# Rotary halves exchanged by VectorE's shuffle instead of by a second set of products, in a two-layer streaming encoder on one core

## The reference

```python
def _rope(x, pos):
    half = x.shape[-1] // 2
    ...
    x1 = x[..., :half].astype(jnp.float32)
    x2 = x[..., half:].astype(jnp.float32)
    return jnp.concatenate([x1 * cos - x2 * sin, x2 * cos + x1 * sin], axis=-1).astype(x.dtype)
...
    q_nope, q_pe = q[..., :MLA_NOPE], _rope(q[..., MLA_NOPE:], pos)
    ckv = _rmsnorm(kv_lat, g_kv_lora)
    kpe = _rope(kpe_raw, pos)
```

## Time and profile before

| | |
|---|---|
| median of 3 runs | 1674.59 us (1674.06 to 1676.32) |
| the profiled execution, its own time | 1674.04 us |
| its span | 1672.2 us |
| busy: TensorE matmuls | 1639.2 us (98%) |
| busy: DVE, ACT, POOL | 1105.0 us (66%), 804.4 us (48%), 576.6 us (34%) |
| heads 0 to 7 | from about 80 us to about 262 us |

### The profile page before, as it was taken

The page is one execution under the profiler, slowest core; times in us unless marked ns, Lnnn a source line. Parts: engine busy times, 40 slices in busy tenths (PEclk is TensorE's granted clock), DMA queues, the critical chain, the costliest instruction groups (busy, mean ns, idle before and its releaser), DMA issues.

```text
span 1672.2 us, 31609 instructions
## 1 busy us (share of the span) xinstructions
PE 1639.2 (98%) x12240; PEld 1589.7 (95%) x12248; DVE 1105.0 (66%) x2047; ACT 804.4 (48%) x1502; POOL 576.6 (34%) x432
## 2 busy tenths in 40 slices
PE   9999999999999999999999999999999999999998
PEld 8989999999998999999999999899989999999998
DVE  5666655555655996587477689533358965874876
ACT  4465555454655654255144445545456541551443
POOL 4453446454553032022013357655550320220122
PEclk9999999999999999999999999999999999999999
DMA  7221223334323133233233322443241332332231
GB/s 193 77 62 53 59 76 98 79 96 108 81 63 80 52 102 114 64 101 104 74 90 88 86 68 69 118 114 89 58 116 52 101 106 71 100 103 76 77 100 58
DMA packets 282744, 145.45 MB, mean 87 GB/s; under 512 B 60334, under 2 KB 273004, under 8 KB 282596
## 3 DMA queue, kind: packets, MB, share of 16 engines
q1 hardware_dynamic: 278136, 136.27, 29.5%
q0 software_dynamic: 3616, 6.92, 1.6%
q10 hardware_dynamic: 844, 0.24, 0.1%
HBM read 130.69 MB, written 15.32 MB: 87 GB/s over the span
## 4 chain that ended last, share of the span: by engine, by line
PE 81%; DVE 11%; ACT 3%; issue 3%; DMA 1%; POOL 1%; SPq 0%; DVEq 0%; ACTq 0%
PE ACC L1269 39%; PE ACC L1682 7%; PE ACC L1684 7%; PE ACC L1683 7%; PE T L1269 3%; PE S L1269 2%; PE ACC L1549 2%; PE S L1524 2%; DVE SCO L2863 2%; DVE TOP L2860 1%; ACT PR L2114 1%; PE S L1684 1%; PE S L1682 1%; PE S L1683 1%; PE T L1537 1%
## 5 line engine op out<-in xcount | busy, mean ns | idle before, releaser
L3502 POOL TENSOR_TENSOR HF<-SG,U 128x576 f32<-128x576 f32 x44 | 65.1, 1478 | 498.4 <-ACT SG L2302 402.3
L1269 PE MATMUL ACC<-XGh,WH 128*128 128x288 f32 (+1 forms) x1008 | 227.6, 307 | 6.7 <-ACT U L2367 2.2
L3347 POOL TENSOR_TENSOR WL<-RAW,WH 128x1024 fp32r<-128x1024 f32 (+3 forms) x84 | 181.4, 2162 | 147.5 <-ACT WH L1989 147.2
L1269 PE MATMUL ACC<-XGh,WL 128*128 128x288 f32 (+1 forms) x1008 | 215.4, 295 | 0.0
L1269 PE MATMUL ACC<-XGl,WH 128*128 128x288 f32 (+1 forms) x1008 | 215.4, 295 | 0.0
L1989 ACT ACTIVATE WH<-RAW 128x1024 fp32r<-128x1024 f32 (+3 forms) x159 | 153.2, 971 | 79.6 <-PE ACC L1269 43.4
L1682 PE MATMUL ACC<-TB,WH 128*128 128x288 f32 x640 | 189.1, 295 | 0.6
L1684 PE MATMUL ACC<-TB,WL 128*128 128x288 f32 x640 | 188.8, 295 | 0.0
L1683 PE MATMUL ACC<-TB,WH 128*128 128x288 f32 x640 | 188.4, 294 | 0.0
L1269 PE MATMUL ACC<-HH,WH 128*128 128x288 f32 x1032 | 179.2, 295 | 0.0
L1269 PEld LDWEIGHTS ACC<-XGh,WH 128*128 128x128 f32 (+1 forms) x1008 | 159.2, 188 | 11.8 <-issue 3.2
(11 more groups left out here) (469 smaller groups left out, 4308.3 us busy)
## 6 DMA issues: line engine op xcount, KB each, us to landing
RAW<-in_w_gate_dram SPq DMA_DIRECT2D x44, 512.0 KB, 3.9
RAW<-in_w_up_dram SPq DMA_DIRECT2D x44, 512.0 KB, 4.6
RAW<-in_w_down_dram SPq DMA_DIRECT2D x32, 512.0 KB, 4.1
RAW<-in_w_in_even_dram SPq DMA_DIRECT2D x29, 512.0 KB, 5.0
RAW<-in_w_in_odd_dram SPq DMA_DIRECT2D x28, 512.0 KB, 4.4
RAW<-in_w_out_even_dram SPq DMA_DIRECT2D x16, 512.0 KB, 4.0
RAW<-in_w_down_dram SPq DMA_DIRECT2D x16, 384.0 KB, 3.5
RAW<-in_w_out_odd_dram SPq DMA_DIRECT2D x8, 512.0 KB, 5.2
```

The lines of the kernel that those rows point to most:

```text
L1269: ins = pe.matmul(out[0:m, 512 * b:512 * b + width], left, right[:, b * width:(b + 1) * width], start=(first and part == 0), stop=(last an ...
L3347: pool.tensor_tensor(WL[slot][:, 0:n], RAW[slot][:, 0:n], WH[slot][:, 0:n].bitcast(F32), ALU.subtract).then_inc(w_lo_pool, 1)
L3502: pool.tensor_tensor(HF[:, q, :], SG[:, q, :], U[:, q, :], ALU.mult).then_inc(h_out, 1)
```

## The change: no second product, a shuffle on VectorE

The columns of the rotary weights, the rows of COS and SIN and the cached keys are laid out so that both halves that change places lie within one group of 32 partitions (16 rows of one and 16 of the other). The product "ps" is gone, and VectorE exchanges the halves of "pe" in PSUM with a stream shuffle. Output tile 5 of heads 3 and 5 stands in slot 4. The key is rotated the same way, its unit is loaded twice as it is, and its columns are reordered as they are split. The store of the latents puts the rotated columns back in order.

```diff
+HALF_SWAP = [(i + SQUARE // 2) % SQUARE for i in range(SQUARE)]
...
-LATENT_TILES = {2: 4, 5: 5, 6: 6, 7: 7}
+LATENT_TILES = {2: 4, 4: 5, 6: 6, 7: 7}
...
-    "even": [("q", 0, 3), ("k", 0, 2), ("v", 0, 2), ("pe", 0, 3), ("ps", 0, 3), None, None, None],
+    "even": [("q", 0, 3), ("k", 0, 2), ("v", 0, 2), ("pe", 0, 3), None, None, None, None],
...
-    "first even": [("q", 0, 3), ("k", 0, 2), ("pe", 0, 3), ("ps", 0, 3), ("v", 0, 2), None, None, None],
+    "first even": [("q", 0, 3), ("k", 0, 2), ("pe", 0, 3), None, ("v", 0, 2), None, None, None],
...
-            unit("pe", g, cols=2 * QLT * P, end=("ps", g))
+            unit("pe", g, cols=QLT * P, end=("pe", g))
...
-            for n, w in enumerate(("k", "v", "pe", "ps", "q")):
+            for n, w in enumerate(("k", "v", "pe", "q")):
...
-    unit_dmas[("kp",)] = 3
+    unit_dmas[("kp",)] = 2
     for n in units.names:
         if n[0] == "pe":
-            unit_dmas[n] = 3 * QLT
+            unit_dmas[n] = 4 * QLT
...
+        def halves_apart(rows):
+
+            return rows.rearrange("p (s q i) -> p q s i", s=2, q=2)
...
-                        sp.dma_start(dst, pe).then_inc(loaded, 16)
-                        sp.dma_start(dsw[:, :, 0:half], pe[:, :, half:ROPE]).then_inc(loaded, 16)
-                        sp.dma_start(dsw[:, :, half:ROPE], pe[:, :, 0:half]).then_inc(loaded, 16)
+                        for h in range(2):
+                            first = (name[1] + h) * (HD + ROPE) + HD
+                            pe = halves_apart(wq[k * P:(k + 1) * P, first:first + ROPE])
+                            for q in range(2):
+                                dst = raw[:, k * P + h * ROPE + q * SQUARE:k * P + h * ROPE + (q + 1) * SQUARE]
+                                sp.dma_start(dst, pe[:, q]).then_inc(loaded, 16)
...
-            sp.dma_start(COS[:, :], a["cos"]).then_inc(rope_in, 16)
-            sp.dma_start(SIN[:, :], a["sin"]).then_inc(rope_in, 16)
+            for dst, src in ((COS, a["cos"]), (SIN, a["sin"])):
+                for o in range(0, P, SQUARE):
+                    rows = src[o // ROPE * ROPE:(o // ROPE + 1) * ROPE, :].rearrange("(s q i) c -> q s i c", s=2, q=2)
+                    sp.dma_start(dst[o:o + SQUARE, :], rows[o // SQUARE % 2]).then_inc(rope_in, 16)
...
-            for o in (0, ROPE):
-                sp.dma_start(CCK[:, KV_LORA + o:KV_LORA + o + ROPE], a["cache_mla_kpe"][0, 0]).then_inc(cc_in, 16)
+            for o in range(0, P, SQUARE):
+                sp.dma_start(CCK[:, KV_LORA + o:KV_LORA + o + SQUARE],
+                             halves_apart(a["cache_mla_kpe"][0, 0])[:, o // SQUARE % 2]).then_inc(cc_in, 16)
...
-                prepare(g, "ps", 0, QLT)
...
+                if name == ("kp",):
+                    old, new = rotary_columns(RAW[slot]), rotary_columns(WH[slot], turned=True)
+                    act.activation(new[:, :, 0], old[:, :, 0], ACT.Copy)
+                    act.activation(new[:, :, 1], old[:, :, 1], ACT.Copy).then_inc(w_hi, 1)
+                    return
...
-                act.wait_ge(acc_free, acc.made("ps", g))
+                act.wait_ge(acc_free, acc.made("pe", g))
...
+            def rotate(out, dst):
+
+                link(dve.tensor_tensor(two(dst), halves(out), two(COS[:, :]), ALU.mult))
+                link(dve.stream_shuffle(halves(out), halves(out), HALF_SWAP))
+                link(dve.tensor_tensor(halves(out), halves(out), two(SIN[:, :]), ALU.mult))
+                return dve.tensor_tensor(two(dst), halves(out), two(dst), ALU.add)
...
-            dve.tensor_tensor(two(YQ[lower, :]), halves(TT)[lower], two(COS[lower, :]), ALU.mult)
-            link(dve.tensor_tensor(two(YK[lower, 0:NT]), halves(TT)[upper], two(SIN[upper, :]), ALU.mult))
-            link(dve.tensor_tensor(YQ[lower, :], YQ[lower, :], YK[lower, 0:NT], ALU.add))
-            dve.tensor_tensor(BO[lower, 0, :], YQ[lower, :], RSTD[lower, :], ALU.mult).then_inc(kp_taken, 1)
-            dve.tensor_tensor(BO[upper, 0, :], YQ[lower, :], RSTD[lower, :], ALU.mult).then_inc(lat_ready, 1)
+            rotate(TT, YQ).then_inc(kp_taken, 1)
+            dve.wait_ge(kp_taken, 1)
+            dve.tensor_tensor(BO[:, 0, :], YQ[:, :], RSTD[:, :], ALU.mult).then_inc(lat_ready, 1)
...
-                    dve.tensor_copy(CKF[0:r, t, :], T[tr.at("lat", t) % 2][0:r, 0:KV_LORA + ROPE]).then_inc(t_free, 1)
+                    out = T[tr.at("lat", t) % 2][0:r, :]
+                    dve.tensor_copy(CKF[0:r, t, 0:KV_LORA], out[:, 0:KV_LORA])
+                    dve.tensor_copy(halves_apart(CKF[0:r, t, KV_LORA:KV_LORA + ROPE]),
+                                    out[:, KV_LORA:KV_LORA + ROPE].rearrange("p (q s i) -> p q s i", q=2, s=2)).then_inc(t_free, 1)
...
-                        ins = dve.tensor_tensor(two(rotated(g)), halves(out), two(COS[:, :]), ALU.mult)
-                    elif what == "ps":
-                        link(dve.tensor_tensor(halves(out), halves(out), two(SIN[:, :]), ALU.mult))
-                        dve.wait_ge(acc_free, acc.made("pe", g))
-                        ins = dve.tensor_tensor(two(rotated(g)), halves(out), two(rotated(g)), ALU.add)
+                        ins = rotate(out, rotated(g))
```

More of the change, by code:

```diff
@@ L341, in plan_attention @@
                 r, what, k0, k1, total = c
-                if k0 == 0 and what not in ("v", "ps") or (k0 == 0 and what == "v" and kind_of(r) != "mla"):
+                if k0 == 0 and what != "v" or (k0 == 0 and what == "v" and kind_of(r) != "mla"):
                     if kind_of(r) != "mla":
@@ L349, in plan_attention @@
                     else:
-                        unit("pe", r, cols=2 * QLT * P, end=("ps", r), in_slot=True)
+                        unit("pe", r, cols=QLT * P, end=("pe", r), in_slot=True)
                 if k1 == total:
@@ L354, in plan_attention @@
                         finished.append((what, r))
-                    elif what in ("q", "v", "ps"):
-                        finished.append(({"v": "kv", "ps": "pe"}.get(what, what), r))
+                    elif what in ("q", "v", "pe"):
+                        finished.append(({"v": "kv"}.get(what, what), r))
             if h < 16 and g is not None and s == k_job_slot(g) == 5:
@@ L845, in last_s, with rotary_columns @@
             return sc.made("s", h, TOK_TILES - 1, 1 if kind_of(h) == "diff" else 0)
+        def halves_apart(rows):
+            return rows.rearrange("p (s q i) -> p q s i", s=2, q=2)
+        def rotary_columns(tile, turned=False):
+            order = "p (m q s i) -> p m q s i" if turned else "p (m s q i) -> p m q s i"
+            return tile[:, :].rearrange(order, q=2, s=2, i=SQUARE // 2)
         def rows_of(t):
@@ L924, in unit_loads @@
                 if w == "kp":
-                    c, r = Q_LORA + KV_LORA, ROPE // 2
-                    return [(0, ROPE, tiles(w_even, 0, DT, c, ROPE)), (ROPE, r, tiles(w_even, 0, DT, c + r, r)),
-                            (ROPE + r, r, tiles(w_even, 0, DT, c, r))]
+                    return [(o, ROPE, tiles(w_even, 0, DT, Q_LORA + KV_LORA, ROPE)) for o in (0, ROPE)]
                 if w == "qi":
@@ L1412, in _ @@
             pe.wait_ge(kp_taken, 1)
-            pe.wait_ge(cc_in, 16 * 3)
+            pe.wait_ge(cc_in, 16 * 5)
             out = rotate_to_tokens(("cc",))
@@ L1444, in prepare @@
                     latent_product(("q", g), ("q", g), 0, P, k0, k1, QLT, QGh, QGl, HALF)
-                elif what in ("pe", "ps"):
-                    latent_product((what, g), ("pe", g), 0 if what == "pe" else QLT * P, P, k0, k1, QLT, QGh, QGl, HALF)
+                elif what == "pe":
+                    latent_product(("pe", g), ("pe", g), 0, P, k0, k1, QLT, QGh, QGl, HALF)
                 else:
@@ L2531, in unit_lo @@
                 slot = slot_of[name]
+                if name == ("kp",):
+                    old, new, high = rotary_columns(RAW[slot]), rotary_columns(WL[slot], turned=True), rotary_columns(WH[slot], turned=True)
+                    dve.tensor_tensor(new[:, :, 0], old[:, :, 0], high[:, :, 0].bitcast(F32), ALU.subtract)
+                    dve.tensor_tensor(new[:, :, 1], old[:, :, 1], high[:, :, 1].bitcast(F32), ALU.subtract).then_inc(w_lo, 1)
+                    return
                 dve.tensor_tensor(WL[slot][:, 0:n], RAW[slot][:, 0:n], WH[slot][:, 0:n].bitcast(F32),
@@ L2629, in _ @@
             begin("kp")
-            dve.wait_ge(rope_in, 16 * 2)
+            dve.wait_ge(rope_in, 16 * 8)
             dve.wait_ge(kp_done, 1)
-            lower, upper = slice(0, ROPE), slice(ROPE, P)
-            dve.tensor_tensor(two(YQ[lower, :]), halves(TT)[lower], two(COS[lower, :]), ALU.mult)
-            link(dve.tensor_tensor(two(YK[lower, 0:NT]), halves(TT)[upper], two(SIN[upper, :]), ALU.mult))
-            link(dve.tensor_tensor(YQ[lower, :], YQ[lower, :], YK[lower, 0:NT], ALU.add))
-            dve.tensor_tensor(BO[lower, 0, :], YQ[lower, :], RSTD[lower, :], ALU.mult).then_inc(kp_taken, 1)
```

(4 more changed lines are left out.)

10 lines of the change are left out of this document (2 added, 8 removed).

## The result

The changed kernel takes 1683.95 us (median of 4 runs, 1681.82 to 1688.74), the kernel before beside it 1674.76: a ratio of 1.006, 95% interval 1.0043 to 1.0078. It is slower by some 9 us. The prediction was 1678.1 us with a range to 1681.5: the right side, and too little. The profiled execution took 1681.82 us with a span of 1680.0, so 7.8 us over the profiled one of before.

A forecast was written before the change was run, and what follows sets the result against it. TensorE, busy 98%, bounds the kernel, but the chain leaves it behind the removed products. +1.0 + 1.2 + 1.2 + 0.1 = +3.5 us on 1674.04, put on the runs' median: 1678.1 us, range 1673.0 to 1681.5.

The forecast's parts named there:

- The shuffle: VectorE's exchange of halves in each rotation: taken as 0.77 us from the stream transpose's row, bounds 0.4 and 1.3 us.
- Head 1: All four rotation operations stand ahead of tile 3's row minima, delaying ScalarE and head 2's scores: +1.0 us.
- Heads 3 and 5: Tile 4's row minima come 2.40 us late, and the next head's first product 1.2 us late: +1.2 us per head.
- Prologue: TensorE's turn stays within 0.3 us, its idle time becomes 3.0 us, second latent copies cost: +0.1 us, between -0.3 and +0.8.
- the key and SyncE's DMAs: Key rotation and extra DMA issues ahead of later loads: costed at nothing, up to +1 us if the DMAs' slack is gone.
- Rival 3: TensorE's clock falls behind idle stretches in prologue and heads 1, 3, 5: +2.4 us once to +9.6, 1680.5 to 1687.7; chance 0.07.
- a dear shuffle: A shuffle of 1.3 us, its excess counted three times, in heads 1, 3 and 5: +1.6 us.
- one fall: One drop of TensorE to 1.2 GHz behind an idle stretch, making the next product take 2.4 us more.
- rival 2: About no change: one of three delays is real, slack in ScalarE and VectorE absorbs the others; 1675 to 1677, chance 0.27.

The follow-up runs named there:

- the first experiment: Changed kernel with unread products on TensorE in its holes (prologue, heads 1, 3 and 5), VectorE's order and all waits kept: 1679.52 us, ratio 1.002.
- The last experiment: The first experiment with the lower half of head 0's odd queries moved on VectorE from slot 0 to slot 4: 1677.92 us, ratio 1.0014.
- The eighth: Changed kernel with 20 unread products on TensorE in the prologue's hole alone, other holes left open: 1682.55 us, ratio 1.0043.
- the second experiment: Changed kernel with the rotation of heads 2, 4 and 6 cut in two on VectorE around the next tile's row minima: 1678.38 us, ratio 1.0013.
- the eleventh: The ninth without its unread products, same orders, holes left open: 1672.68 us, ratio 0.9982.
- the ninth: The fifth with unread products of heads 3 and 5 moved to tile 3's score bank and head 0's odd lower half to slot 4: 1670.95 us, ratio 0.9975.
- fifth: Changed kernel with the rotation cut in two, VectorE reordered in the prologue and heads 3 and 5, and remaining holes filled with unread products: 1675.40 us, ratio 0.9998.
- sixth: Kernel before the change with only two VectorE reorderings, in the prologue and for output tile 6 in heads 3 and 5: 1675.62 us, ratio 0.9997.

## Why the prediction was wrong

**The shuffle: right.** Forecast 0.77 us, measured 0.76 in all five places, and the load of its mask takes 0.01. The Trainium skill, "VectorE: DVE Perf Modes", section "The perf-mode tier table", gives some 2400 ns for 2048 columns; the 0.87 us that I had estimated from it are 0.11 us too dear here.

**Head 1: right, link by link.** Take off the 2.45 us by which head 1 begins later: the minima of tile 3 at 107.22 (forecast 107.23), the exponent of tile 4 at 113.18 - 2.45 = 110.73 (110.85), the scores of head 2 at 113.29 (113.35, being 112.32 + 1.03). +0.97 us for +1.0.

**Heads 3 and 5: right.** With 5.71 us taken off, PTh of tile 3 starts at 156.74 (forecast 156.79) and the first product of head 4 at 167.40 - 5.71 = 161.69 (161.74). In the first experiment, where only waits are left, that product starts at 164.15, 3.0 us late with the 0.6 taken off, of which 1.9 had come before head 3: 1.1 us for 1.2.

**Prologue: the wait right, what follows not.** TensorE's turn stays at 77.06 (77.09), its hole is 2.91 us (3.0). I had priced it at +0.1, and with the hole filled it costs nothing (80.47 less 0.6, 79.86 before). Its true price is the next step's. The terms that I had put at nothing ahead of it, the key and SyncE's DMAs, cost nothing: TensorE's first wait stands at 64.84 us, 64.80 before.

**The clock: the step that failed.** The sum priced only waits and took the full clock behind every hole. In the trace the falls cost 3.8 us, more than the 3.5 us of the whole forecast. Rival 3, "the clock falls", had a chance of 0.07, on the ground that the clock is full in every slice and "no row shows a longer one". But no row could: the kernel before has no wait over 0.6 us in these stretches, so its trace said nothing for or against. Nor is "full in every slice" what the row says: a 9 stands for 0.90 or more over 42 us, and the changed kernel, with four falls, has a 9 in every slice too. I had even listed the four holes that the change would dig and their lengths (3.0 us, and 2 to 3 in pieces); all four came, and the clock fell behind all four. The size was off too. I had 2.4 us for each fall. Measured are 1.5 in the prologue (79.86 to 81.33) and 2.3 in head 2 (139.54 - 115.74 against 133.83 - 112.32); the other two cost nothing in this trace, because there the slower products of output tiles 6 and 7 run beside the chain over VectorE that sets the first product of the next head. With the holes filled TensorE waits 0.79 us for that chain at the first product of head 4, and from head 3's first scores to the second tile of head 4 it takes 30.3 us in both traces. The Trainium skill, "TensorE: Matmul & The Clock Gate", section "Part 1: The HAM clock gate", says that idleness brings the clock to half and activity brings it back; the windows above agree (0.50 between 115 and 120 us, 1.00 again from 125), and the first experiment shows cause and effect.

**Head 0: a term that was missing.** +1.0 us, in no step of mine. VectorE's lower half of the odd queries, and beside it GpSimd's split of a weight, in the kernel before and in the changed one:
```profile
82.51 0.75 DVE L2727 TENSOR_TENSOR QPO<-BO,QPO 64x576 fp32r<-64x576 f32 x1
...
82.63 1.52 POOL L3347 TENSOR_TENSOR WL<-RAW,WH 128x384 fp32r<-128x384 f32 x1 [2.28 <-ACT WH L1989]
```
```profile
84.10 1.01 POOL L3367 TENSOR_TENSOR WL<-RAW,WH 128x384 fp32r<-128x384 f32 x1 [3.79 <-ACT WH L2002]
...
84.11 1.61 DVE L2748 TENSOR_TENSOR QPO<-BO,QPO 64x576 fp32r<-64x576 f32 x1
```
Before, VectorE came first and GpSimd took 1.52 us for what takes 1.01; after, GpSimd came first by 0.01 us and VectorE paid with 0.86. The last experiment moved it away and got 1.6 us back, 1.3 of them in head 0. The eighth shows the collision alone. Its prologue and head 0 are the first experiment's, where both instructions start at 83.25 us and VectorE takes 1.62. In its trace both start together too, and this time VectorE got through:
```profile
83.08 0.75 DVE L2759 TENSOR_TENSOR QPO<-BO,QPO 64x576 fp32r<-64x576 f32 x1
...
83.08 1.63 POOL L3378 TENSOR_TENSOR WL<-RAW,WH 128x384 fp32r<-128x384 f32 x1 [2.35 <-ACT WH L2013]
```
Head 0 lasts 13.52 us there, 14.37 in the first experiment and 13.38 in the kernel before. So 0.85 of the 1.0 us hang on which of two instructions comes first in a tie. VectorE paid in seven traces with the change and this order, GpSimd in one. The Trainium skill, "SBUF — State Buffer", section "Who interferes with whom", has it so: a VectorE operation with both inputs in SBUF contends with a GpSimd operation that reads SBUF, the lock on their shared ports is exclusive, and the order of issue decides who waits. The traces agree: the later one ends 1.61 to 1.63 us after the common start, where both together take 1.76.

**The sum.** Waits: 1.0 (head 0) + 1.0 + 1.2 + 1.2 = 4.4 us at head 7's scores in the first experiment (234.21 - 0.6 - 229.24), forecast 3.5 without head 0. Clock: 1.5 + 2.3 = 3.8. Together 8.2, as the table has it, where I had +3.5 in the sum: too little by 1.0 for head 0 and by 3.8 for the clock, and 0.1 too much in the prologue. The median of the runs lies another 2.1 us above the profiled one (in the kernel before 0.7); the run at 1688.74 us has a mean clock of 0.990, the profiled one 0.993. Which stretches fell there no trace shows.

**The range.** Its upper end is not the sum of what it names: 1678.1 + 1.6 (a dear shuffle) + 1.0 (SyncE) + 2.4 (one fall) are 1683.1, not 1681.5; and rival 2's 1675 less 1.1 are 1673.9, not 1673.0. The measured 1683.95 lies outside either way. The side was right for a reason that holds, the waits. That the first experiment's runs leave 3.8 us beside a forecast of 3.5 is partly luck: its trace has 4.4 us, 1.0 of them in head 0, which was in no step of mine.

## What to carry to other kernels

Work taken from a busy engine comes back only where that engine doesn't wait behind the taken piece. Otherwise it becomes a hole, and on TensorE a hole has a price of its own: the clock. Where a change opens holes, count a fall of the clock as a likely case, not as a remote one. Between 60 and 270 us of these traces, the clock fell behind 15 of 16 holes of 2.4 us and more (head 1's pair taken as one), and behind one of ten of 1.0 to 1.9 us. When an operation grows on VectorE, ask which tile's row minima stand behind it, and cut it in two around them. A trace that has no such hole is no evidence on what one does, and slices of 42 us hide falls of a few microseconds.

## What the hardware did that I had not expected

The same hole does not always do the same. The hole of 1.90 us in head 1 was followed by a lower clock in the second experiment (0.71) and by none in the eleventh; the hole in head 5 by one in the changed kernel (2.74 us, 0.66 from 210 to 215 us) and by none in the eighth experiment (2.75 us). And at the end of the first layer's heads stands a hole of 1.17 us that nothing in this study touches. The kernel before has it as well, at 541.59 us, far behind the rows that the prediction read. In the eleventh experiment, TensorE's wait there, the pace behind it and the window:
```profile
538.86 0.44 PE L1619 MATMUL T<-MIXh,WH 128*128 128x288 f32 x1 [1.17 <-ACT MIXh L2259]
539.10 0.44 PE L1619 MATMUL T<-MIXh,WL 128*128 128x288 f32 x1
```
```profile
530.00:560.00 30.00, 28.76 (x204) 27.96 (x203) 19.29 (x28) 18.35 (x28) 4.90 (x4) 0.94 0.19 54
```
and in the ninth:
```profile
538.55 0.37 PE L1630 MATMUL T<-MIXh,WH 128*128 128x288 f32 x1 [1.18 <-ACT MIXh L2274]
538.76 0.29 PE L1630 MATMUL T<-MIXh,WL 128*128 128x288 f32 x1
538.89 0.29 PE L1630 MATMUL ACC<-MIXh,WH 128*128 128x288 f32 x1
```
```profile
530.00:560.00 30.00, 28.74 (x215) 27.94 (x214) 21.11 (x29) 18.46 (x28) 4.59 (x4) 1.00 0.24 70
```
In the second, fifth, sixth and eleventh experiments' traces the clock is 0.94 in this window, in those of the kernel before, the changed one and the ninth it is 1.00. The sixth experiment is the kernel before in another order, with neither the change nor unread products. So most of the 1.7 us between the profiled executions of the ninth and the eleventh experiment is a fall at a place that neither of them changes. That the unread products ahead of it make it rarer is not shown. Of the change itself the same holds: that its holes bring the clock down is shown by filling them, but an execution need not fall at all four places, as head 5 of the eighth experiment shows.
